# An earlier place for one weight rounding at the end of attention, and a later one for three small transposes

## What is computed

```python
h = _rmsnorm(x, g_pre) * (1.0 + scale) + shift
q, k, v, f, u, bg, cg, ga, gb = _split_cols(h @ w_in, IN_SIZES)
logf = jax.nn.log_sigmoid((f + b_f).astype(jnp.float32))
...
a = o.reshape(B, T, D_ATTN) @ w_oa
b = (bg * y_conv) @ w_ob
m = (jax.nn.sigmoid(ga) * a + jax.nn.sigmoid(gb) * b) @ w_o
x = x + gate1 * _rmsnorm(m, g_post1)
...
return x + gate2 * _rmsnorm(f, g_post2)
```

## Time and profile before

| | |
|---|---|
| median of 3 runs | 1841.3 us (1840.64 to 1842.74) |
| profiled execution | time 1839.91 us, span 1838.1 us |
| TensorE busy | 1806.4 us, 98% of the span |
| DVE, ACT busy | 875.1 us (48%), 704.8 us (38%) |
| mean of what DMA moved | 208 GB/s |
| chain that ended last | TensorE 95%, DVE 2%, ACT 1%, DMA 1% |

### The profile page before, as it was taken

How to read it: one execution, slowest core, us unless ns; L and a number is a source line. 1 busy time by engine, 2 the same in 40 slices (tenths; PEclk the granted TensorE clock), 3 DMA queues, 4 the chain that set the end, 5 groups by cost and what they waited for, 6 DMA issues and landing times.

```text
span 1838.1 us, 31832 instructions
## 1 busy us (share of the span) xinstructions
PE 1806.4 (98%) x13703; PEld 1684.8 (92%) x13703; DVE 875.1 (48%) x1041; ACT 704.8 (38%) x817; POOL 26.7 (1%) x77
## 2 busy tenths in 40 slices
PE   8999999999999999999999999999999999999997
PEld 4889978887589999999969999999999999999996
DVE  4456743334644343453365434444444445566565
ACT  3423222334643333343354233333333334555453
POOL 0001000010000000000000000000000000000000
PEclk9999999999999999999999999999999999999999
DMA  9987878864665555449847464444444445544441
GB/s 344 386 320 247 301 266 331 319 252 167 230 207 161 164 170 169 160 144 352 318 170 252 138 251 161 160 162 169 170 161 160 160 162 173 169 161 161 162 160 52
DMA packets 189591, 382.37 MB, mean 208 GB/s; under 512 B 8789, under 2 KB 9261, under 8 KB 189199
## 3 DMA queue, kind: packets, MB, share of 16 engines
q1 hardware_dynamic: 185744, 378.04, 58.8%
q0 software_dynamic: 1328, 2.58, 0.4%
q10 hardware_dynamic: 2424, 0.37, 0.2%
HBM read 376.15 MB, written 4.81 MB: 207 GB/s over the span
## 4 chain that ended last, share of the span: by engine, by line
PE 95%; DVE 2%; ACT 1%; DMA 1%; issue 1%; SPq 0%; DVEq 0%; ACTq 0%
PE bank L566 29%; PE bank L568 28%; PE bank L567 28%; PE bank L576 4%; PE bank L771 1%; PE bank L905 1%; DMA ada<-in_w_ada 1%; DMA x_rows<-in_x_sample 1%; PE bank L584 1%; PE bank L874 0%; PE bank L622 0%; PE bank L824 0%; DVE xT L2027 0%; PE bank L841 0%; ACT w_hi L1074 0%
## 5 line engine op out<-in xcount | busy, mean ns | idle before, releaser
L566 PE MATMUL bank<-a_lo,w_hi 128*128 128x288 f32 x3648 | 1085.4, 298 | 5.7 <-DVE a_lo L1642 3.2
L567 PE MATMUL bank<-a_hi,w_hi 128*128 128x288 f32 x3648 | 1076.8, 295 | 0.0
L568 PE MATMUL bank<-a_hi,w_lo 128*128 128x288 f32 x3648 | 1073.0, 294 | 0.0
L1507 DVE TENSOR_TENSOR w_lo<-raw,w_hi 128x2048 fp32r<-128x2048 f32 x244 | 559.3, 2292 | 742.2 <-ACT w_hi L1074 741.4
L1074 ACT CAST w_hi<-raw 128x2048 fp32r<-128x2048 f32 x244 | 465.5, 1908 | 833.7 <-PE bank L568 826.8
L566 PEld LDWEIGHTS bank<-a_lo,w_hi 128*128 128x128 f32 x3648 | 684.1, 188 | 24.1 <-issue 18.0
L568 PEld LDWEIGHTS bank<-a_hi,w_lo 128*128 128x128 f32 x3648 | 687.6, 188 | 0.0
L567 PEld LDWEIGHTS bank<-a_hi,w_hi 128*128 128x128 f32 x3648 | 685.6, 188 | 0.0
L576 PE MATMUL bank<-ada,cT 128*32 128x512 f32 x544 | 63.1, 596 | 2.7 <-DMA ada<-in_w_ada 2.7
L1606 DVE TENSOR_TENSOR a_lo<-hid,a_hi 128x1152 fp32r<-128x1152 f32 x44 | 59.4, 1352 | 12.3 <-ACT a_hi L1104 12.3
L1104 ACT CAST a_hi<-hid 128x1152 fp32r<-128x1152 f32 x44 | 50.8, 1156 | 0.0
(11 more groups left out here) (290 smaller groups left out, 936.9 us busy)
## 6 DMA issues: line engine op xcount, KB each, us to landing
raw<-in_w_ffn_in SPq DMA_DIRECT2D x88, 1024.0 KB, 4.9
raw<-in_w_in SPq DMA_DIRECT2D x80, 1024.0 KB, 7.2
ada<-in_w_ada SPq DMA_DIRECT2D x68, 1024.0 KB, 9.9
raw<-in_w_ffn_out SPq DMA_DIRECT2D x44, 1024.0 KB, 5.1
ada_o<-in_w_ada SPq DMA_DIRECT2D x26, 1024.0 KB, 9.5
raw<-in_w_o SPq DMA_DIRECT2D x16, 1024.0 KB, 5.6
raw<-in_cache_k SPq DMA_DIRECT2D x16, 512.0 KB, 4.4
raw<-in_cache_v SPq DMA_DIRECT2D x16, 512.0 KB, 4.1
```

Of the source, the lines that this page charges most:

```text
L566: pe.matmul(acc, w_hi[buf][:, a, cols], lo[:, kt, :], start=first and a == 0, stop=False)
L567: pe.matmul(acc, w_hi[buf][:, a, cols], hi[:, kt, :], start=False, stop=False)
L568: mm = pe.matmul(acc, w_lo[buf][:, a, cols], hi[:, kt, :], start=False, stop=last and a == SK - 1)
L1507: tt(w_lo[buf][:, :, :], raw[s][:, :, :], w_hi[buf][:, :, :].bitcast(F32), ALU.subtract).then_inc(raw_turn, 1)
```

## The change

Two steps move.

First, turn_lf goes from behind slot 1 to behind slot 3 of q, k and v on TensorE, and copy_lf on DVE from turn 2 to turn 4, directly ahead of new_sums.

Second, ACT rounds the first gated slot in turn s = 6 (SB - 2) between exp_sample(6) and copy_o_s(5), and not in turn 7 behind copy_pT(7, 0); the four waits in front go along. DVE's split_lo of this slot moves ahead of sample_lo(6), into turn 7. Nothing is added or taken out; SP's and POOL's orders are the same.

```diff
@@ TensorE, the q, k and v slots
-                if u == 1:
+                if u == 3:
                     turn_lf()
@@ ScalarE, attention's turns
                 exp_sample(s)
-                copy_o_s(s - 1)
-                copy_pT(s, 0)
-                copy_KT(s + 1, 0)
-                if s == SB - 1:
+                if s == SB - 2:
 
                     act.wait_ge(s_out, 16 * 6)
                     act.wait_ge(sS_ps, SB - 1)
                     act.wait_ge(O_ps, SB // 2)
                     split_hi(N_MIX, 0, R_MIX + 1, 0)
+                copy_o_s(s - 1)
+                copy_pT(s, 0)
+                copy_KT(s + 1, 0)
                 copy_pT(s, 1)
@@ VectorE, the q, k and v slots
-                if u == 2:
+                if u == 4:
                     copy_lf()
-                if u == 4:
                     new_sums()
@@ VectorE, attention's turns
                 norm_sample(s)
+                if s == SB - 1:
+                    split_lo(N_MIX, 0, 0)
                 sample_lo(s - 1)
-            split_lo(N_MIX, 0, 0)
             pair_lo(SB - 1)
```

## The result

The change made the kernel slower: 1846.4 us (median of 8, 1845.0 to 1846.9) against 1841.1 us (median of 8, 1840.6 to 1842.7), a ratio of 1.0027 with a 95% interval of 1.0016 to 1.0038. The forecast was 1847.5 in 1844.6 to 1851.0. A second set gave 1845.9 against 1841.7, 1.0021 (1.0012 to 1.0030).

The account below looks back on a forecast made before the run. TensorE, busy in nearly all slices, was taken to bound the kernel. The terms 10.1 - 3.3 - 1.5 + 2.6 - 1.7 gave +6.2 us on 1841.3, so 1847.5 us, range 1844.6 to 1851.

Parts of the forecast that it names:

- Term 1: In the q, k and v stage, TensorE's wait for z_rows ahead of the lf transposes goes: -1.7 us.
- Term 2: In the seventh turn, ScalarE's rounding waits for its late load, delaying copy_o_s(5) and TensorE's turn_k(7): +10.1 us.
- Term 3: From turn_k(7) to the first gated product, the stretch shortens without the rounding in its old place: -3.3 us.
- Term 4: In the first gated product's first quarter, the old stall and its low clock are gone: -1.5 us.
- Term 5: From turn_k(7) on, TensorE's clock is half for a while behind the new stall: +2.6 us.
- The first: Seventh turn: no wait for the load or the copies, so the change is faster, 1834.8 us; chance 0.04.
- The second: q, k and v stage: late DMA queues give back the lf gain, all else as forecast, 1849.2 us; chance 0.06.
- The third: Clock stays at 1.2 GHz from turn_k(7) until the dense products, 1855.7 us; chance 0.07.
- The fourth: Seventh turn: the wait is there but shorter, result within 0.2% of before, at 1844 us or less; chance 0.05.

## Why the prediction was right

- **Term 1, lf, -1.7.** Right. The wait is gone (254.35 to 256.01 before, nothing now). In the changed kernel's profile it shows as -1.44, since the slots began 0.28 us later, and in that of the lf part alone as -1.7 ahead of the seventh turn. The slack of the loads was there. The median of the lf part alone, -2.3, is no proof of the size: its interval, -3.5 to -0.2, holds -1.7 and also the -0.8 by which its first gated product was sooner. What I hadn't seen: alone, it brings ScalarE to the rounding ahead of the load and loses about 0.9 us again there.
- **Term 2, the wait, +10.1.** Right in its mechanism, its place and its size: 9.97 in the profile, L771 for o_s, and the first load's issue as the gate, shown by the early load (stall 4.7) and the later place (4.9).
- **Term 3, the old place, -3.3.** 13.37 us became 11.92 with the clock half for 4.0 of them, which is 9.9 at full clock: -3.4. With the clock kept up it took 10.0 us, where 10.1 was worked out. w_lo was the last thing that the product waited for, as worked out.
- **Term 4, the old stall's clock, -1.5.** Mis-sized. Its profile has 1.3, but with the clock kept up the kernel before gained 3.2 in the medians (1.5 to 4.8). I took one profiled execution for the rule; three profiles have 1.3, 1.4 and 4.2 us. This can be most of what the forecast was too high by, 0.9 us in one set and 1.9 in the other.
- **Term 5, the new stall's clock, +2.6.** Right mechanism, a little large: TensorE worked at half clock from 506.91 to 510.9, 2.0 us; the kernel with the clock kept up is 1.9 us quicker over this stretch and 2.6 in the medians.
- With 10.0 - 3.4 - 1.7 + 2.0 and -1.3 to -3.2 for term 4 the sum is +5.6 to +3.7, and the two sets measured +5.3 and +4.3. The profile has +5.7 up to the last matmul of the products. The bounds, added up, reach 1849.8 us, a little over the 1849 that the prediction gives; the stated range covers it.
- **The rivals.** The first (no wait) is out by the 10.1 us row. The second (lf given back) is out by the -1.44 ahead of the seventh turn, and by the lf part alone, which waits for nothing there. The third (clock low up to the products) is out: the clock was back at 510.9, 8 us ahead of the first product, in a turn that is half transposes. The Trainium skill ("TensorE: Matmul & The Clock Gate", Part 4) says that TensorE's full clock doesn't engage for transposes. This trace doesn't agree: from 506.91 up to the clock's rise at 510.9 TensorE ran nothing but transposes (L771, L841, L918, L919), and the clock stayed up behind it. The fourth needed a landing 2.5 us sooner; it came 6.8 us after the issue and not 7.1.

## What to carry to other kernels

Before a step is moved up in an engine's order, look up when what it waits for is issued, on the queue that issues it, and what stands behind the step on its own engine. Here an early place paid only once the load had moved up as well: the change cost 4 to 5 us with the late load in turn 6, and with the early load and a place in turn 7 the whole set of moves brought 7.6. And price a stall of TensorE with its clock, from several executions and not from one.

## What the runs showed of the hardware

- After nearly the same stall of 2.2 to 2.3 us TensorE ran at 1.2 GHz for 3, 7 or 10 us in three profiles, and the fall came 0.8 us before the stall's end in one and about 2 us behind it in two. It cost 1.4, 1.3 and 4.2 us.
- The clock rose from 1.2 to 2.4 GHz while TensorE ran only transposes, 4.0 us after it had begun them behind the stall of 10.1 us (506.91 to 510.9).
- Whether that is what spreads the executions stays open. Those of before lie within 2.1 us in a set of 8 and within 4.1 to 5.4 in the sets of 15 to 27, those with the early load alone (10) within 6. Those without a longer gap lie within 1.7 to 2.7 (5 to 11), but so do those with split_lo alone (11), whose first gap is the same, and those of the changed kernel (8 and 11) within 1.9.
- Filling the gaps of 2.3 and about 1 us with nine idle matmuls was worth 3.2 us in the medians (1.5 to 4.8), though the first product didn't start sooner.
- A load of 1 MB, issued at the same place of the program, landed between 6.6 and 8.0 us later in ten profiles. Issued about 8 us sooner, right behind k's pages, it took 8.5 to 9.2 us in three.
